# A second attention whose long rows come in the order 3, 2, 0, 1, and exponentials ahead of copies in its last short unit

## The reference

```
def chunk_causal_attention(q, k, v):            # 8 heads, q and k 96 wide, v 64 wide
    for qb in range(S // 128):
        q0 = qb * 128
        L = q0 + 128
        s = einsum('bhqd,bhkd->bhqk', q[:, :, q0:L], k[:, :, :L]) * dk ** -0.5
        s = where(s_chunk <= t_chunk, s, -inf)
        p = softmax(s, axis=-1)
        outs.append(einsum('bhqk,bhkd->bhqd', p, v[:, :, :L]))
```

## Time and profile before

| | |
|---|---|
| timed runs | median 1508.63 us of 3 (1504.21, 1508.63, 1508.82) |
| profiled execution, its own time | 1502.07 us |
| its span, first to last instruction | 1500.3 us |
| second attention in that span | about 497 to 661 us |
| mean granted TensorE clock | 0.982 |

### The profile page before, as it was taken

How to read it: one execution, slowest core, us unless ns; L and a number is a source line. 1 busy time by engine, 2 the same in 40 slices (tenths; PEclk the granted TensorE clock), 3 DMA queues, 4 the chain that set the end, 5 groups by cost and what they waited for, 6 DMA issues and landing times.

```text
span 1500.3 us, 21082 instructions
## 1 busy us (share of the span) xinstructions
PE 1417.3 (94%) x7433; PEld 1088.5 (73%) x7433; DVE 970.1 (65%) x1755; ACT 855.4 (57%) x1550; POOL 136.9 (9%) x205
## 2 busy tenths in 40 slices
PE   6999999999999989999999999977999999999996
PEld 5888999544445544458878888766888888888885
DVE  5513216367649866767763343357888988988887
ACT  6321467366657656653252333334777788888876
POOL 1000000122300200000000000000111111111211
PEclk9999999999999999999999999996999999999998
DMA  6231124420020001021120001235996666666694
GB/s 225 49 124 43 60 88 173 175 102 1 1 112 1 1 2 55 29 92 49 43 113 28 29 32 54 68 134 193 352 361 207 213 218 217 222 217 219 225 367 145
DMA packets 89396, 189.01 MB, mean 126 GB/s; under 512 B 14313, under 2 KB 24553, under 8 KB 88562
## 3 DMA queue, kind: packets, MB, share of 16 engines
q1 hardware_dynamic: 80050, 166.11, 31.1%
q0 software_dynamic: 7200, 22.03, 5.7%
q10 hardware_dynamic: 2080, 0.01, 0.1%
HBM read 218.54 MB, written 28.31 MB: 165 GB/s over the span
## 4 chain that ended last, share of the span: by engine, by line
PE 76%; DMA 8%; DVE 8%; ACT 5%; issue 3%; POOL 1%; DVEq 0%; ACTq 0%; SPq 0%; POOLq 0%
PE psum L1999 31%; PE psum L2241 17%; PE psum L1983 8%; DMA up_stage<-in_w_up 7%; PE psum L2136 6%; PE psum L2159 4%; PE psum L2118 4%; PE psum L1976 3%; DVE up_rest L1652 3%; DVE gate_rest L1652 1%; PE psum L2408 1%; ACT arena L1186 1%; ACT arena L1341 1%; ACT up_high L1202 1%; POOL arena L778 1%
## 5 line engine op out<-in xcount | busy, mean ns | idle before, releaser
L890 ACT ACTIVATE arena<-psum 128x512 f32<-128x512 f32 (+3 forms) x193 | 84.5, 493 | 87.0 <-PE psum L2159 52.0
L1652 DVE TENSOR_TENSOR down_rest<-down_stage,down_high 128x1024 fp32r<-128x1024 f32 x96 | 115.0, 1218 | 29.4 <-ACT down_high L1202 29.4
L1652 DVE TENSOR_TENSOR up_rest<-up_stage,up_high 128x1024 fp32r<-128x1024 f32 x100 | 117.0, 1219 | 15.3 <-ACT up_high L1202 15.0
L2136 PE MATMUL psum<-arena 64*128 64x512 f32 (+7 forms) x384 | 115.4, 519 | 11.1 <-ACT arena L1167 9.0
L1537 DVE TENSOR_TENSOR_SCAN arena<-arena,singles 128x768 f32<-128x768 f32 (+7 forms) x64 | 86.3, 1363 | 55.6 <-POOL arena L778 45.9
L1983 PE MATMUL psum<-arena 128*128 128x512 f32 (+2 forms) x352 | 118.0, 487 | 0.8 <-DVE arena L1522 0.8
L1652 DVE TENSOR_TENSOR gate_rest<-gate_stage,gate_high 128x1024 fp32r<-128x1024 f32 x100 | 115.7, 1217 | 0.3
L1999 PE MATMUL psum<-up_high,rows_high 128*128 128x256 f32 x384 | 110.2, 287 | 5.7 <-DVE up_rest L1652 5.3
L1202 ACT ACTIVATE up_high<-up_stage 128x1024 fp32r<-128x1024 f32 x100 | 100.3, 1059 | 23.9 <-DMA up_stage<-in_w_up 23.8
L1999 PE MATMUL psum<-up_rest,rows_high 128*128 128x256 f32 x384 | 108.6, 283 | 0.0
L1999 PE MATMUL psum<-up_high,rows_rest 128*128 128x256 f32 x384 | 108.6, 283 | 0.0
(11 more groups left out here) (408 smaller groups left out, 3487.8 us busy)
## 6 DMA issues: line engine op xcount, KB each, us to landing
gate_stage<-in_w_gate SPq DMA_DIRECT2D x25, 2048.0 KB
up_stage<-in_w_up SPq DMA_DIRECT2D x25, 2048.0 KB
down_stage<-in_w_down SPq DMA_DIRECT2D x24, 2048.0 KB
arena<-in_x SPq DMA_DIRECT2D x16, 512.0 KB, 3.5
arena<-in_w_mkv SPq DMA_DIRECT2D x8, 1024.0 KB, 6.4
arena<-in_w_in SPq DMA_DIRECT2D x4, 1024.0 KB, 10.7
arena<-in_w_mo SPq DMA_DIRECT2D x4, 1024.0 KB, 6.4
mv_times_w_mo_spill<-arena SPq DMA_DIRECT2D x8, 512.0 KB, 2.8
```

Source lines behind the costliest of these rows:

```text
L890: do(act.activation(dst, src, ACT.Copy), s_te["act"])
L1652: ins = dve.tensor_tensor(split[part][1][:, k, :], stage[part][:, k, :], split[part][0][:, k, :].bitcast(F32), ALU.subtract)
L2136: mm = pe.matmul(scores_of(kind, n)[:, at:end], lhs, rhs(at, end), start=True, stop=True)
```

## The change

Long units after the first take their rows in the order 3, 2, 0, 1; unit 4 keeps 0, 1, 2, 3. Rows 3 and 2 of the long units have two buffers, rows 0 and 1 one buffer each, at addresses written out in `LONG_AT`. An exponential of row 0 or 1 in units 5 to 7 waits for that row's last transposition in the unit before (after block 4 or 5), every other exponential for the last transposition of the unit before the last. In unit 3 the exponentials of unit 4 move: row 0 ahead of block 0, row 1 in block 0, rows 2 and 3 in block 1, 4 and 5 in block 2, 6 and 7 in block 3; and within blocks 0 and 1 the copies of the heads come behind the first exponential instead of ahead of both. The order of TensorE's instructions in unit 3 is the same. In the first attention nothing changes but the form of the code.

```diff
-FIRST = {"sb": 1, "mla": 0}
+LONG_ROWS = (3, 2, 0, 1)
 def row(kind, n):
     u, k = divmod(n, ROWS)
-    first = 1 if kind == "sb" or u < PAIRS else 0
-    return u, (k // 2 + first) % GRP, k % 2
+    r = (k // 2 + 1) % GRP if kind == "sb" or u < PAIRS else k // 2 if u == PAIRS else LONG_ROWS[k // 2]
+    return u, r, k % 2
...
-             ("mla", "last short"): {j: (2 * j, 2 * j + 1) for j in range(4)}}
+             ("mla", "last short"): {-1: (0,), 0: (1,), 1: (2, 3), 2: (4, 5), 3: (6, 7)}}
...
-def last_row(kind, r):
-    return r == (FIRST[kind] + GRP - 1) % GRP
+def last_row(r):
+    return r == 0
...
-        p_long = row_buffers("mla", 36864, 43520)
+        LONG_AT = {(3, 0): 36864, (2, 0): 38912, (0, 0): 40704, (1, 0): 42752, (3, 1): 44288, (2, 1): 46336}
+        def p_long(u, r, a):
+            n = P * (GRP + r + 1)
+            return cut(LONG_AT[r, u % 2 if r >= 2 else 0] + n * a, n)
...
-                        if kind == "mla" and j >= 0 and late_heads(u, j):
-                            up_turned(late_heads(u, j), T - 1)
-                        for k in steps.get(j, ()) if more else ():
+                        for i, k in enumerate(steps.get(j, ()) if more else ()):
                             one(ROWS * (u + 1) + k)
+                            if kind == "mla" and i == 0 and j >= 0 and late_heads(u, j):
+                                up_turned(late_heads(u, j), T - 1)
...
-                before_ = u - 1 if u >= PAIRS and last_row("mla", r) else u - 2
-                if before_ >= 0:
-                    act.wait_ge(s_t, LAST["mla", before_] + 1)
+                if u > PAIRS and r < 2:
+                    act.wait_ge(s_t, ROUND["mla", u - 1, GRP + r, 1] + 1)
+                elif u >= 2:
+                    act.wait_ge(s_t, LAST["mla", u - 2] + 1)
```

## The result

The changed kernel takes 1497.82 us (median of 8 runs, 1495.50 to 1500.01) against 1507.63 for the kernel before (8 runs, 1503.80 to 1513.42); ratio 0.9936, 95% interval 0.9919 to 0.9952. Two later comparisons gave 0.9945 (0.9929 to 0.9960) and 0.9959 (0.9945 to 0.9972). Over the 19 executions of the changed kernel in these three comparisons and the 77 of the kernel before in the three sets of runs that came later the means are 1498.7 and 1506.4, 7.8 us apart. The forecast was 1503.3, 5.3 us less, with a range from 1499.0: the direction was right, the size too small, and the time lies 1.2 us under the range.

What follows compares the result with a forecast made beforehand. The prediction took TensorE, busy for 94% of the span, to bound the kernel. Its terms 3.29 + 1.52 + 0.47 = 5.3 us, taken off 1508.63, gave 1503.3 us, with a range of 1499.0 to 1507.7.

Steps and rivals of the forecast that it cites:

- the base: Starting level of the whole kernel's time: median of three timed runs, 1508.63 us, 6.6 above the profiled execution.
- the clock: End of unit 6: the granted clock's fall costs 1.7 us, about the same after the change, left out of the sum.
- the signs in the profile: No idle time at named scores in units 3 to 6, one 2.1 us break before unit 7, starting 5.5 us earlier.
- Bound by TensorE and its breaks: Second attention: runs at TensorE's own pace with short breaks, all on the path that sets the end.
- Part 1: Unit 3: exponentials ahead of blocks and heads remove TensorE's breaks of 1.68 and 1.61 us, 3.29 us in sum.
- Part 2: Units 4 and 5: row order 3, 2, 0, 1 with new buffers removes a 0.76 us wait in each, 1.52 us.
- The slack I gave for the wide exponential: Long units, exponential 0: taking 1.12 instead of 0.78 us leaves 0.6 of 0.95 us slack, so it costs nothing.
- Part 3: End of unit 6: narrower last row shortens the final chain by 0.62 us, less 0.15 given back; net 0.47 us.
- the 0.15 given back by the mix operations: End of unit 6: ScalarE's two mix operations end some 0.15 us too late for unit 7's first copy.
- A: Rival: the clock stays at 2.4 GHz at the end of unit 6, 1.7 us more gain, 1501.6 us; chance 0.24.
- B: Rival: unit 3's breaks move to score 5 instead of going; gain only 3.4 us, 1505.2 us; chance 0.2.
- C: Rival: late wide exponentials delay each block of the long units, 7.2 us lost, slower at 1510.5 us; chance 0.06.

Runs made afterwards that it cites:

- the order alone: Kernel before with only the new order of exponentials and copies in unit 3, long rows and buffers as they were; 1502.00 us, ratio 0.9970.
- the long rows alone: Changed kernel with the order of exponentials and copies in unit 3 put back as before; 1502.76 us, ratio 0.9978 to the kernel before.
- the delayed one: Changed kernel with 28 identity matmuls (6.15 us) between the second attention and the w_o product; 1506.79 us, ratio 0.9998 to the kernel before.
- the same program filled in unit 3: Kernel before with 21 identity matmuls, results unused, in the four breaks of unit 3; 1505.82 us, ratio 0.9994.
- The run with exponentials 4 and 6 ahead: Changed kernel with exponentials 4 and 6 computed in unit 3 moved ahead of the copies of blocks 2 and 3; 1499.04 us, ratio 0.9955.

## Why the prediction was wrong

The forecast lay 5.5 us above the measured 1497.82. By means, 2.2 of that come from the base, 1.0 from breaks and scores of the attention that were sized too small (6.3 in the corrected span, 6.13 in the profile, where 5.3 was forecast) and 1.4 from the clock. The last 0.9 is how the 8 executions of the first comparison fell. So two steps failed, the base and the clock, and the signs in the profile all came: no idle time before scores 2 and 4, none at the first scores of units 6 and 7, one break before unit 7, whose start comes 5.6 us earlier (5.5 forecast).

**Bound by TensorE and its breaks:** right. Nearly every microsecond won in the attention is one of the breaks read in the earlier trace rows, and the parts, made alone, add up.

**Part 1, 3.29 us:** right; the order alone made the attention 3.37 shorter, score 2 stands at 0.89 us behind the turn's start and score 4 at 5.25 behind score 2, with no idle time. Score 5 waits 0.1 us, as forecast.

**Part 2, 1.52 us:** the mechanism was right, the term a little too small. Units 4 and 5 are 1.67 shorter. To the start of unit 4 the forecast had 2.0 and the trace 2.29. Half of the difference is in each part: with the order alone unit 4 starts 3.44 earlier instead of 3.29, and with the long rows alone 1.16 later instead of 1.30. The second is probably because the last score there had waited for an exponential as well, too briefly for a row of its own (0.05 us idle before it), and the wide score before it now covers that. The slack I gave for the wide exponential held (no idle time at score 2, 567.48).

**Part 3, 0.47 us:** the shorter last row was right (unit 6 by 1.95, forecast 1.92), the 0.15 given back by the mix operations did not come. Unit 7 is 0.22 shorter; why is open. In sum the attention gave 6.13 where 5.28 was forecast.

**The base:** this step failed. "The three timed runs have a median 6.6 us higher, 1508.63, and I take the same difference off that" takes the median of three executions for the level; 77 executions have a median of 1506.1 and a mean of 1506.4. So the range, which ended 4.3 under the forecast, stood too high by more than 2 us: from 1506.4, with everything else as it was, it would have reached down to 1496.8 and held the measured time.

**The clock:** this step failed too. "I leave the clock out of the sum" held at the end of unit 6, where the slow stretch is 1.7 us of loss in both kernels. It left out two other places. One is the router, where the logits took 1.93 us in four traces of the changed kernel and 2.85 to 3.31 in four of the kernel before, 1.1 us between the profiled ones. That the change shifts them to a better place fits these eight traces and the delayed one; the same program filled in unit 3 had both lengths, and shifts of 3.4 and 7 us did not bring it. So this microsecond was luck of the place, not a profit of the mechanism, and how often it comes is not settled. The other is unit 3. Behind its first break the clock fell in one of four traces of the kernel before, 3.3 us; the profiled one had no fall, and I argued from it that breaks of 1.68 pass. One in four would be 0.8 us on average, an estimate from a single fall; filling these breaks won nothing that the runs can tell (0.9994). 6.1, 1.1 and 0.8 make 8.0, near the 7.8 between the means, but the timed runs show only that 1.4 of it lies in the loss.

**The rivals:** the range held A, 1.7 us of clock, and nothing for clock effects elsewhere. A was nearest in time and wrong in place: the clock still falls at the end of unit 6. B and C did not happen.

The Trainium skill, page "TensorE: Matmul & The Clock Gate", section "Architectural detail: the array is 16x 32x32, not 1x 128x128", says that ScalarE works strictly in order. The run with exponentials 4 and 6 ahead agrees: exponential 6 waits for its bias until 559.80, and the copies of block 3, whose transpositions are done at 560.15, start only behind it, at 560.90. That lateness cost TensorE no idle time; the 0.32 us left of the 1.00 is the wait for the exponential itself, whose bias came at 559.80.

## What to carry to other kernels

When one engine bounds a kernel and waits at unit boundaries, order the units' rows so that the wide ones come first and narrower ones last, double the buffers of the wide ones and give single ones to those that come free early. The breaks then go as the idle times in the timeline say; here every part came within 0.4 us. Put small work that is ready ahead of copies that are not. Take the level that a forecast starts from out of more than three executions when the effect is as small as their spread. And do not forecast from one trace whether the clock falls behind a break: price a fall at every break about as long as those that had one behind them here. One of 1.35 us near 417 us, with 0.31 soon behind it, had a fall in 15 of the 18 traces. Price it also far behind the change, where only the position moves.

## What the runs showed of the hardware

- Behind a break of 1.69 us, with 0.40 idle shortly ahead of it, the clock fell from 2.4 to 1.2 GHz in one execution and not in three others of the same program. The two slow pieces cost 2.64 and 0.63 us.
- Behind a break of 2.16 us the clock fell in all seven traces that had it. Nine matmuls of the identity (18 instructions) in it kept the clock at 1.00 in each of the three traces that had them (111.45, 110.09 and 110.09 us for the attention). Started at 1.2 GHz, the same 18 took 3.92 instead of 2.27 us.
- The stretch up to the turn of the last heads took 542.4 to 543.0 us in some traces and 544.7 to 545.9 in others, with an additional slow piece near 370 us in all but one of the longer ones: 2.5 us that come with either kernel, ahead of everything that the change touches, and are as large as most effects looked for here.
- The same 16 matmuls of the router's logits took 1.93 to 3.41 us, by whether the clock fell 2.1 us or more behind their start or 0.2 us behind it.
